# The high half of the weights moves from ScalarE to VectorE, and two scalings of the mLSTM move to ScalarE

## What is computed

```python
def squared_relu_mlp(h, w1, w2):
    return jnp.square(jax.nn.relu(h @ w1)) @ w2

def odd_mixer(h, C0, n0, m0, w_in, gate_b, head_norm_g, w_out):
    ...
    hh, Cm, n, m = mlstm_chunked(...)
    hh = rmsnorm(hh, head_norm_g) * jax.nn.sigmoid(o_pre.reshape(B, L, H_C, DV_C).astype(jnp.float32))
    out = hh.reshape(B, L, V_C).astype(h.dtype) @ w_out
    ...

# a step of mlstm_chunked: decayed keys update the state, the numerator is divided by the denominator
    num = w_inter[..., None] * jnp.einsum('bhid,bhdv->bhiv', q_c, Cm) + jnp.einsum('bhij,bhjv->bhiv', s, v_c)
    h = num / jnp.maximum(jnp.abs(den), jnp.exp(-m_t))[..., None]
    Cm = keep[..., None, None] * Cm + jnp.einsum('bhj,bhjd,bhjv->bhdv', wk, k_c, v_c)
```

## Time and profile before

| | |
|---|---|
| median of three runs | 2792.64 us |
| the profiled execution | 2790.7 us |
| its span, first to last instruction | 2789.0 us |
| TensorE matmuls busy | 2699.6 us, 97% |
| VectorE busy | 1378.1 us, 49% |
| ScalarE busy | 1166.0 us, 42% |
| GpSimd busy | 214.5 us, 8% |
| mean granted TensorE clock | 0.986 |

### The profile page before, as it was taken

How to read it: one execution, slowest core, us unless ns; L and a number is a source line. 1 busy time by engine, 2 the same in 40 slices (tenths; PEclk the granted TensorE clock), 3 DMA queues, 4 the chain that set the end, 5 groups by cost and what they waited for, 6 DMA issues and landing times.

```text
span 2789.0 us, 40745 instructions
## 1 busy us (share of the span) xinstructions
PE 2699.6 (97%) x17004; PEld 2400.1 (86%) x17004; DVE 1378.1 (49%) x2162; ACT 1166.0 (42%) x2020; POOL 214.5 (8%) x350
## 2 busy tenths in 40 slices
PE   7999999999999999999999999999999999999997
PEld 5779888888888879889999998997777797999996
DVE  4645554644554546534444446534554447443335
ACT  5554446454645335433234345434332344333323
POOL 5111101100000000110000001110000000000000
PEclk9999999999999999999999999999999999999998
DMA  6443223522323335652332425544443334343231
GB/s 187 154 121 97 86 68 100 167 72 87 91 69 92 91 95 152 189 159 79 113 104 84 120 78 163 172 138 119 125 129 118 121 100 139 95 130 112 86 91 67
DMA packets 367062, 317.93 MB, mean 114 GB/s; under 512 B 11245, under 2 KB 338987, under 8 KB 366880
## 3 DMA queue, kind: packets, MB, share of 16 engines
q1 hardware_dynamic: 336224, 207.91, 25.7%
q0 software_dynamic: 30656, 107.43, 12.2%
HBM read 260.35 MB, written 54.94 MB: 113 GB/s over the span
## 4 chain that ended last, share of the span: by engine, by line
PE 77%; issue 10%; DVE 5%; ACT 5%; DMA 2%; POOL 0%; ACTq 0%; DVEq 0%; POOLq 0%
PE dense L543 64%; PE mixer L543 10%; ACT arena L1040 1%; DVE wlo L1524 1%; ACT whi L1040 1%; PE mixer L776 1%; DMA arena<-mrow 1%; DMA wst<-in_w_ff_dram 0%; DVE hf L1662 0%; ACT L1040 0%; ACT hhi L1040 0%; DVE hlo L1658 0%; ACT relu L1040 0%; ACT ffh L1040 0%; DVE arena L1957 0%
## 5 line engine op out<-in xcount | busy, mean ns | idle before, releaser
L543 PE MATMUL dense<-hhi,whi 128*128 128x272 f32 (+1 forms) x3072 | 853.2, 332 | 27.1 <-DVE hlo L1658 10.2
L543 PE MATMUL dense<-hhi,wlo 128*128 128x272 f32 (+1 forms) x3072 | 828.3, 324 | 0.0
L543 PE MATMUL dense<-hlo,whi 128*128 128x272 f32 (+1 forms) x3072 | 826.8, 324 | 0.0
L1524 DVE TENSOR_TENSOR wlo<-wst,whi 128x1024 fp32r<-128x1024 f32 x384 | 469.9, 1224 | 254.7 <-ACT whi L1040 254.1
L543 PEld LDWEIGHTS dense<-hhi,whi 128*128 128x128 f32 x3072 | 517.7, 189 | 87.0 <-issue 26.8
L1040 ACT ACTIVATE whi<-wst 128x1024 fp32r<-128x1024 f32 x384 | 404.2, 1053 | 426.4 <-PE dense L543 396.3
L543 PEld LDWEIGHTS dense<-hhi,wlo 128*128 128x128 f32 x3072 | 516.2, 190 | 42.5
L543 PEld LDWEIGHTS dense<-hlo,whi 128*128 128x128 f32 x3072 | 518.2, 190 | 37.1 <-issue 1.0
L543 PE MATMUL dense<-h1hi,whi 128*128 128x272 f32 (+1 forms) x1536 | 424.6, 331 | 12.6 <-DVE wlo L1524 6.9
L543 PE MATMUL dense<-h1lo,whi 128*128 128x272 f32 (+1 forms) x1536 | 414.5, 324 | 0.0
L543 PE MATMUL dense<-h1hi,wlo 128*128 128x272 f32 (+1 forms) x1536 | 414.0, 324 | 0.0
(11 more groups left out here) (318 smaller groups left out, 1865.9 us busy)
## 6 DMA issues: line engine op xcount, KB each, us to landing
wst<-in_w_ff_dram SPq DMA_DIRECT2D x256, 512.0 KB, 3.9
wst<-in_w_in_even_dram SPq DMA_DIRECT2D x48, 512.0 KB, 3.9
wst<-in_w_in_odd_dram SPq DMA_DIRECT2D x48, 512.0 KB, 3.9
proj<-ffh POOLq DMA_DIRECT2D x48, 272.0 KB, 2.4
proj<-ffh POOLq DMA_DIRECT2D x48, 256.0 KB, 2.3
arena<-proj POOLq DMA_DIRECT2D x8, 1536.0 KB, 10.5
wst<-in_w_out_even_dram SPq DMA_DIRECT2D x16, 512.0 KB, 4.1
wst<-in_w_out_odd_dram SPq DMA_DIRECT2D x16, 512.0 KB, 3.7
```

The costliest lines, as they stand in the source:

```text
L543: return pe.matmul(out, lhsT, rhs, start=start, stop=stop)
L1524: TT(wlo[:, u % 2, :], wst[:, u % 2, :], whi[:, u % 2, :].bitcast(F32), ALU.subtract)\
```

## The change

`hi` moves from ScalarE's program to VectorE's as a `tensor_copy`, called at the end of VectorE's `unit_begin(u)`, so at `("d", u, 0)` behind `h1_rest`; the first unit's copy moves from `("pr", 0, 0)` to `("pr", 0, 1)`. Its waits and its semaphore stay. ScalarE takes the scaling of the keys (`mA`), one activation for each head, and of the results (`mD`), where a new semaphore `g_fac` tells it that the factor is there. The sample tile's version of `mD` stays on VectorE.

```diff
@@ ScalarE
-            def hi(u):
-                if u >= len(PLAN.units):
-                    return
-                if u >= 1:
-                    act.wait_ge(S("w_used"), u)
-                act.wait_ge(S(f"w_loaded{u % 2}"), 16 * (u // 2 + 1))
-                A_(whi[:, u % 2, :], wst[:, u % 2, :], ACT.Copy).then_inc(S("w_hi"), 1)
...
-                if step == "mB":
+                if step == "mA":
+                    w("kT")
+                    for h in range(H):
+                        last = A_(m["KW"][0:n, h], M4(1)[0:n, h], ACT.Copy, scale=cum[0:n, t, 4 + h:5 + h])
+                    s(last, "kw")
+                elif step == "mB":
...
                     head_rms(t, n)
+                    w("fac")
+                    for h in range(H):
+                        last = A_(m["HN"][:, h], MB[:, h, 0:DV], ACT.Copy, scale=small[:, 7, h:h + 1])
+                    s(last, "on")
...
-                if item == ("pr", 0, 0):
-                    hi(0)
                 if item[0] == "d":
-                    if item[2] == 0:
-                        hi(item[1] + 1)
@@ VectorE
+            def hi(u):
+                if u >= len(PLAN.units):
+                    return
+                if u >= 1:
+                    dve.wait_ge(S("w_used"), u)
+                dve.wait_ge(S(f"w_loaded{u % 2}"), 16 * (u // 2 + 1))
+                dve.tensor_copy(whi[:, u % 2, :], wst[:, u % 2, :]).then_inc(S("w_hi"), 1)
...
                 if kind == "f1" and k or kind == "f2" and k == 0:
                     h1_rest(u - 1)
+                hi(u + 1)
...
                 if step == "mA":
-                    w("kT")
-                    s(TT(m["KW"][0:n], M4(1)[0:n], bcl(wk, [n, H, P]), ALU.mult), "kw")
                     if n == NS:
+                        w("kT")
...
                 elif step == "mD":
                     head_scale(t)
-                    for h in range(H):
-                        last = dve.tensor_scalar(m["HN"][:, h], MB[:, h, 0:DV], small[:, 7, h:h + 1], None, ALU.mult)
-                    s(last, "on")
+                    dve.sem_inc(S("g_fac"), 1)
...
                 if item == ("pr", 0, 1):
+                    hi(0)
                     lo(0)
```

## The result

The changed kernel takes 2798.66 us, the median of 20 runs (2792.60 to 2805.22), beside 2792.91 us in 20 runs of the kernel before (2787.34 to 2798.48). The ratio is 1.002 with a 95% interval of 1.0011 to 1.0029. So the change costs 5.8 us, 3.1 to 8.1 by the interval. The forecast was 2792.6 us and a difference within 0.2%, 5.6 us. The time lies in the stated range and the difference at the edge of the likeliest case, but it is a loss, where gains and losses were to cancel.

What follows compares the result with a forecast made beforehand. TensorE, busy 97%, was taken to bound the kernel, with helper-engine order at single hand-offs deciding. Gains of 8.4 us and losses of 8.4 us cancel at 2790.7 us profiled, 2792.6 us as median; 8-in-10 range 2782 to 2802.

Steps and rivals of the forecast that it cites:

- Neither sign of being wrong: The prediction is wrong if TensorE's waits for wlo exceed 20 us, or ScalarE's HN scalings take over 0.6 us each.
- The DeltaNet term: DeltaNet tiles starting beside projections: VectorE is packed, one copy falls into each of four tiles, a loss of 2.4 us.
- the 0.7: Gain from the other six waits for wlo: two of them end on ScalarE's copy and give 0.7 us.
- I cost this half at zero: Scalings moved to ScalarE: TensorE's g_on comes as late as before, within 0.2 us either way over eight tiles.
- The cover of 0.8 us: Undisturbed f1 unit of group 0: wlo ends 0.4 us later after the change, still 0.8 us before TensorE needs it.
- The close hand-offs: Six hand-offs, 1629.48 to 2349.39, where TensorE starts within 0.5 us of wlo's end: 6 x 0.6 = 3.6 us lost.
- the term of 1.2 us: First f1 unit, behind the norm: the second hlo starts at about 539.1 instead of 537.86, a loss of 1.2 us.
- the clock term: First f1 unit: whether the granted clock falls there was left open, 0 to 1.7 us, and taken as 0.
- The second: Rival: VectorE ends the hand-off, once some 20 of 256 MLP units have a side operation: 2801 us, chance 0.13.
- The first: Rival: ScalarE's relief is worth more than counted, losses shrink to 3, two more half-clock stretches go: 2784 us, chance 0.24.
- The third: Rival: the copy runs at full rate, 1.22 us, because it rounds; losses grow, gains shrink: 2801.5 us, chance 0.08.
- The fourth: Rival: the fast copy holds up GpSimd's transfers, some seven late by one copy, 4.8 us: 2797.5 us, chance 0.05.

Runs made afterwards that it cites:

- full-rate copy: Changed kernel with VectorE making the high half by a maximum of wst with itself instead of the copy: 2824.24 us, ratio 1.0116.
- VectorE in the first stage alone: Against the kernel before, VectorE copies units 0 to 56, ScalarE the rest, and the scalings stay on VectorE: 2787.93 us, ratio 0.9973.
- the early split: Changed kernel with the next unit's copy and wlo both ahead of h1_rest in MLP units: 2784.04 us, ratio 0.9968 against the kernel before.

## Why the prediction was right and wrong, point by point

**The prices.** Right for the two moved operations. The copy took 0.696 us, against 0.69; the results' scaling 0.475, against 0.48. In the undisturbed `f1` unit of the changed kernel

```profile
1011.43 0.60 ACT L1040 ACTIVATE relu<-dense 128x512 f32<-128x512 f32 x1 [6.21 <-PE dense L543]
...
1013.40 0.69 DVE L1545 TENSOR_TENSOR h1lo<-relu,h1hi 128x512 fp32r<-128x512 f32 x1 [2.27 <-ACT relu L1040]
1014.01 0.69 DVE L1523 CAST whi<-wst 128x1024 fp32r<-128x1024 f32 x1
1014.73 1.23 DVE L1529 TENSOR_TENSOR wlo<-wst,whi 128x1024 fp32r<-128x1024 f32 x1
```

`wlo` ends 4.53 us after the Relu's start; in the earlier trace rows it was 4.13. That is the 0.4 later of the sum. VectorE's busy time was foretold as 1643 us less the scalings, some 1624, and is 1599.4, because of the overlap told above. Neither sign of being wrong came: TensorE waits 11.4 us for `wlo`, and the `HN` scalings take 0.475 us. The first watched one tile, and the loss came in others too.

**The gains.** Right at the places named: the waits at 52 and 125 us are gone, that at 142 us is 2.80 (2.7 was said), that at 1025 us 1.44 (1.4 was said), that at 1426 us 0.34. The window of 50 to 60 us, at a clock of 0.83 in the earlier trace rows, is now at full clock:

```profile
50.00:60.00 10.00, 10.00 (x57) 8.07 (x57) 6.67 (x10) 7.07 (x13) 0.54 (x1) 1.00 0.64 178
```

Not all of it stays. The later start, 1.1 us in the sum, can't be told from scatter: unit 1 begins 0.8 us later, but 1.1 later with the scalings alone. TensorE's waits for `ffh` grow from 7.9 to 9.5 us in all although the one at 142 us shrinks by 0.95: evacuations that were hidden behind the late split now end waits of their own. The sum had no term for that.

The DeltaNet term, 2.4 us, lies in this stage too, and it was too high. TensorE's waits on that step rose from 2.4 to 4.9, which looks like it. Of the two waits, the one at 310.84 before, 1.08 us, is 2.15 at 305.20 in the changed kernel. It is 2.1 to 2.7 in every kernel with VectorE's copy there and 1.1 in the two where ScalarE copies these units, so this rise of 1.1 us is the copy's. The other rise is not. Here it is before, in the changed kernel, and with the scalings alone, where ScalarE copies:

```profile
383.17 1.05 PE L543 MATMUL mixer<-arena 128*128 128x128 f32 x7 [1.28 <-DVE arena L1780]
```

```profile
377.43 0.95 PE L543 MATMUL mixer<-arena 128*128 128x128 f32 x3 [2.77 <-DVE arena L1786]
```

```profile
385.34 0.94 PE L543 MATMUL mixer<-arena 128*128 128x128 f32 x6 [2.77 <-DVE arena L1789]
```

With VectorE's copy in all projections it is 1.29 us. What makes it 1.5 us longer or shorter is open; the copy it is not.

In sum the terms made some 3 us up to unit 56 (5.2 for the first 150 us less 2.4, and a part of the 0.7); with the copy alone there, the runs gave 5.9, a part of it clock.

**The losses.** Here the sum failed. The copy from unit 57 on costs 8.3 us in the runs, its gains there set off. The terms for that part made 3.6 + 1.8 + 0.6 = 6.0 less the 1.0 at 1025 us, so 5.0 (the 1.5 at 1426 us is the scaling's and not in that kernel). In the whole change, the loss at hand-offs and behind them was short, at the steps below. The one that failed most is the last: what else stands behind the copy on VectorE was put at next to nothing. It fails with the copy alone too.

- "I cost this half at zero ... VectorE's part of the hand-off has more than that", of the results' scaling on ScalarE. The Relu was to come up to 0.5 us later; at 1624.26 it starts 1.7 us behind the factor, since it stands behind all four scalings. The cover of 0.8 us was read from an undisturbed unit and used for all, though 1629.48 was one of the prediction's own six places without cover, and it stands at an `mD` step. The scaling costs 1.9 us there. The gain at 1426 us, which was counted as 1.5, pays for it, so the scalings together come to nothing within their interval. Zero was right for TensorE's `g_on` and wrong for the hand-off.
- The close hand-offs were 3.6 us, six times one copy. All new or grown waits for `wlo` came to 5.7, with the one above in it; with the copy alone they are 3.0. The mechanism and the size were right, the places in part others.
- One `h1lo` late by a copy was counted as a loss of 0.6. TensorE's two waits for `h1lo`, 2.0 us before, are gone in the changed kernel: one behind a wait for `wlo` in the same unit that grew from 1.80 to 2.24, the other with the scalings, as it is gone with the scalings alone.
- What stands behind the copy on VectorE was searched for `wlo`, `hlo`, `h1lo` and DeltaNet alone. TensorE's waits for the evacuations into `accA` (3.1 to 5.1 us), for the norms' sums (3.9 to 4.8 us) and for the state of the sample group in the mLSTM (line 2004, 0.7 to 1.9 us) were at nothing in the sum beyond one 0.6. They grew by 4.1 us together, and by as much with the copy alone (5.3, 4.8 and 1.9 us). The full-rate copy, which lengthens nothing but the copy, takes them to 9.2, 8.5 and 2.9 us.

**The first `f1` unit.** A wait of over 2 us was foretold; the longest is 1.65. Behind the unit's first matmul TensorE's waits for `hlo` total 3.4 us, as before (3.6), so the term of 1.2 us did not come as a wait. The unit is 1.4 us longer all the same, and that is near the term by luck: TensorE stands 3.4 us in it against 3.6, and is busy 9.1 against 7.4. This is the clock term which the prediction had taken as zero with a bound of 1.7: the granted clock is 0.62 from 536 to 543 us, so at 1.2 GHz for a good part of it, and it fell behind these waits. Only a part of it can be the copy's, since with the scalings alone and with VectorE in the first stage alone, where ScalarE makes this unit's copy, TensorE is busy 8.5 and 8.4 us in it.

```profile
536.00:543.00 7.00, 6.71 (x18) 4.63 (x19) 4.99 (x8) 2.56 (x5) 0.00 (x0) 0.62 0.51 150
```

**The rivals.** The second is the nearest to what came: VectorE ends the hand-off, and exchanging the copy with `h1_rest` takes the loss away. It was to decide from some 20 places with a side operation, at 0.6 us each, for 8.4 us; it came with 5.8 in all, from five more close units and from what stands behind the copy. The first fell: the relief of ScalarE is in the first stage alone. The third fell by the copy's row, and its price was far too low: 8.9 us were given for a full-rate copy, 25.6 measured, because a cover of 0.8 us was taken to hold at 0.27. The fourth came as a mechanism and not as a time. GpSimd's instructions that issue transfers take longer beside fast copies (busy us, mean ns | idle us before); before, changed kernel, full-rate copy:

```profile
L2187 POOL DMA_DIRECT2D proj<-ffh x96 | 52.4, 547 | 606.2 <-ACT ffh L1040 422.3 <-DVE ffh L1566 183.8 <-issue 0.2
```

```profile
L2191 POOL DMA_DIRECT2D proj<-ffh x96 | 54.4, 567 | 603.1 <-ACT ffh L1040 420.7 <-DVE ffh L1571 182.2 <-issue 0.2
```

```profile
L2191 POOL DMA_DIRECT2D proj<-ffh x96 | 52.5, 547 | 608.9 <-ACT ffh L1040 427.4 <-DVE ffh L1571 181.3 <-issue 0.2
```

All 275 of them take 180.9, 188.1 and 180.9 us. One by one, 23 are over 0.1 us longer than before, each of them beside a copy, the longest by 0.56 us, which is under one copy. The stores of 272 and 256 KB land after 2.6 and 2.5 us, against 2.4 and 2.3 before and 2.5 and 2.4 with the full-rate copy. None of it shows in TensorE's waits, and the full-rate copy, which leaves GpSimd's issues as they were, was slower and not faster.

## What to carry to other kernels

Before an operation moves to an engine with room, write out what then stands in one row behind the last outside event. Here it was square, `h1lo`, copy, `wlo`, of which only `h1lo` needs the square; the loss was in the order, not in the engine, and putting the independent work first turned +5.8 us into -9.9, against -5.9 with VectorE's copy in the first stage alone; the runs don't part these two, so what is shown is that with this order the MLP loses nothing on VectorE. A cover read at an undisturbed place says nothing of the places that have none, so price a change at those, and list everything behind the moved operation, evacuations and sums included.

## What the runs showed of the hardware

**Rounding keeps the doubled rate.** The copy from fp32 to fp32r ran 1024 columns in 0.696 us, against 1.22 us for the two-input form of the same work. The condition that the Trainium skill gives in "VectorE: DVE Perf Modes", section "What auto-detection actually checks", a single source and a destination both in SBUF, held into fp32r as well.

**The fast copy and GpSimd hold each other up.** Of the 384 copies of the changed kernel, 318 lay beside no GpSimd instruction, and none of these took over 0.70 us. Of the 66 others, 7 took over 0.85 us, the longest this one:

```profile
1970.46 1.42 POOL L2348 DMA_DIRECT2D arena<-proj  x1 [44.86 <-DVE hlo L1974]
1970.86 1.51 DVE L1523 CAST whi<-wst 128x1024 fp32r<-128x1024 f32 x1
```

With the early split one took 2.33 us beside GpSimd's memsets at the start. The full-rate form took 1.20 to 1.23 us in all 384. By the Trainium skill, "SBUF — State Buffer", section "Who interferes with whom", whoever issues first has the shared port and the other blocks; the prediction had weighed only one of the two orders. It costs little here: the 66 took 0.742 us on average and the others 0.687, so 66 x 0.055 = 3.6 us of VectorE's time, against the 7.2 us of GpSimd's told above.

**Half-clock stretches come and go between executions.** After the wait at 1628.96 the clock is 0.57 over 4 us, so mostly at 1.2 GHz, in the changed kernel:

```profile
1630.00:1634.00 4.00, 4.00 (x20) 3.97 (x20) 1.50 (x2) 0.00 (x0) 0.00 (x0) 0.57 0.76 229
```

Such a stretch costs about 1.6 us of progress. Over units 40 to 47 TensorE is busy 68.4 us in the kernel before, whose clock falls once there, and 66.8 us with the scalings alone, whose clock does not; it stands 3.6 us in both. So units gain or lose that amount also where no wait differs. The 20 runs of the changed kernel scatter from 2792.6 us at a mean clock of 0.987 to 2805.2 us at 0.981, so an effect of 6 us can only be seen in medians.
